# An MoE decoder step on one Trainium2 core: each expert's first matrix as one 4 MB transfer instead of two of 2 MB

## What is computed

```python
def expert_block(args):
    xb, e = args
    gu = xb @ w_e_in[e]                        # (1024, 1024): 4 MB in float32
    gt, up = jnp.split(gu, 2, axis=-1)
    return (jax.nn.silu(gt) * up) @ w_e_out[e]   # (512, 1024): 2 MB in float32

out = lax.map(expert_block, (buf.reshape(n_blocks, MOE_BLOCK, D_MODEL), block_expert)).reshape(-1, D_MODEL)
y = jnp.sum(out[dest].reshape(T, EXP_TOPK, D_MODEL).astype(f32) * gate[..., None], axis=1)
```

## Time and profile before

| | us |
|---|---|
| median of 3 runs | 1650.59 (1649.15 to 1651.14) |
| the profiled execution | 1654.85 |
| its span, first to last instruction | 1653.0 |
| stage with the experts, fetches and blocks in turn | about 1121.5 to 1612 |
| TensorE busy | 1494.1 (90% of the span) |
| chain that ended last | PE 66%, DMA 21%, DVE 6%, issue 3% |

### The profile page before, as it was taken

How to read it: one execution, slowest core, us unless ns; L and a number is a source line. 1 busy time by engine, 2 the same in 40 slices (tenths; PEclk the granted TensorE clock), 3 DMA queues, 4 the chain that set the end, 5 groups by cost and what they waited for, 6 DMA issues and landing times.

```text
span 1653.0 us, 34687 instructions
## 1 busy us (share of the span) xinstructions
PE 1494.1 (90%) x14388; PEld 1195.1 (72%) x14388; DVE 692.1 (42%) x1226; ACT 454.5 (27%) x873; POOL 170.7 (10%) x355
## 2 busy tenths in 40 slices
PE   7999899999999999999999899948887886978887
PEld 7999799999988899999888598724443443434443
DVE  5766576666688562223443243651111110101115
ACT  4533554544322641222433322111000000000000
POOL 0000000000000000000000000013232232323320
PEclk9999899999999999999999999969899998989999
DMA  5222445344457223352464726538999999699994
GB/s 205 71 82 89 112 151 152 110 145 143 148 203 268 79 90 102 119 181 89 150 226 147 280 74 252 226 163 352 421 403 422 371 421 422 254 405 419 420 389 165
DMA packets 86705, 368.64 MB, mean 223 GB/s; under 512 B 14280, under 2 KB 37520, under 8 KB 71568
## 3 DMA queue, kind: packets, MB, share of 16 engines
q1 hardware_dynamic: 80432, 357.76, 57.0%
q0 software_dynamic: 6144, 8.95, 1.5%
HBM read 345.20 MB, written 29.31 MB: 227 GB/s over the span
## 4 chain that ended last, share of the span: by engine, by line
PE 66%; DMA 21%; DVE 6%; issue 3%; ACT 2%; SPq 1%; POOL 1%; POOLq 0%; DVEq 0%; ACTq 0%
PE ps L619 33%; DMA arena<-in_w 13%; PE ps L760 5%; DMA xg<-x_dram,curg 5%; PE ps L1077 4%; PE ps L1096 4%; PE ps L973 3%; PE ps L865 3%; PE ps L847 3%; PE ps L712 1%; PE ps L709 1%; DVE cv L1650 1%; PE ps L1061 1%; PE ps L876 1%; DMA kv<-in_vc 1%
## 5 line engine op out<-in xcount | busy, mean ns | idle before, releaser
L1077 PE MATMUL ps<-arena,xT 128*32 128x256 f32 x4096 | 255.4, 402 | 55.7 <-DMA arena<-in_w 55.0
L1589 DVE TENSOR_TENSOR wl<-raw,wh 128x1024 fp32r<-128x1024 f32 x152 | 184.6, 1222 | 166.2 <-ACT wh L1154 166.0
L619 PE MATMUL ps<-xh,wh 128*128 128x272 f32 x1136 | 245.0, 297 | 5.5 <-DVE wl L1589 5.5
L1077 PEld LDWEIGHTS ps<-arena,xT 128*32 128x32 f32 x4096 | 132.7, 114 | 153.5 <-DMA arena<-in_w 42.2
L619 PE MATMUL ps<-xh,wl 128*128 128x272 f32 x1136 | 235.2, 289 | 0.0
L619 PE MATMUL ps<-xl,wh 128*128 128x272 f32 x1136 | 234.5, 288 | 0.0
L619 PEld LDWEIGHTS ps<-xh,wh 128*128 128x128 f32 x1136 | 179.6, 189 | 17.2 <-issue 13.2
L619 PEld LDWEIGHTS ps<-xl,wh 128*128 128x128 f32 x1136 | 178.7, 189 | 0.0
L619 PEld LDWEIGHTS ps<-xh,wl 128*128 128x128 f32 x1136 | 177.7, 189 | 0.0
L1154 ACT ACTIVATE wh<-raw 128x1024 fp32r<-128x1024 f32 x152 | 159.1, 1055 | 38.9 <-PE ps L973 20.8
L2232 DVE TENSOR_TENSOR hbuf<-sg,ps 128x128 f32<-128x128 f32 x64 | 18.4, 288 | 300.7 <-ACT sg L1454 235.1
(11 more groups left out here) (404 smaller groups left out, 2402.0 us busy)
## 6 DMA issues: line engine op xcount, KB each, us to landing
arena<-in_w SPq DMA_DIRECT2D x96, 2048.0 KB
raw<-in_slabs SPq DMA_DIRECT2D x152, 512.0 KB, 4.4
bc<-acs_dram SPq DMA_DIRECT2D x16, 512.0 KB, 5.8
hs<-in_h SPq DMA_DIRECT2D x16, 512.0 KB, 5.3
out_h_sample<-hs SPq DMA_DIRECT2D x16, 512.0 KB, 4.1
kv<-in_kT SPq DMA_DIRECT2D x8, 1024.0 KB, 4.8
kv<-in_vc SPq DMA_DIRECT2D x4, 1024.0 KB, 7.8
kvx<-in_vc SPq DMA_DIRECT2D x2, 2048.0 KB, 11.4
```

Of the source, the lines that this page charges most:

```text
L619: r = nc.tensor.matmul(ps[:, 2 * (ub % 2) + half, 0:HT], w[:, s, col], x[:, koff + kk, half * HT:half * HT + HT], start=first and kk == 0 ...
L1077: r = nc.tensor.matmul(ps[QS * c:QS * c + QS, 2, 0:2 * FQ], xT[:, s, kk % 2, kk // 2 * QS:kk // 2 * QS + QS], arena[:, at_:at_ + 2 * FQ], ...
L1589: v.tensor_tensor(wl[:, s], raw[:, s], wh[:, s].bitcast(F32), ALU.subtract).then_inc(w_lo, 1)
```

## The change

Each first matrix is fetched as one transfer with one semaphore, and `gate_up` waits for it once, before step 0. The same is done in the conditional part for blocks that don't fit.

```diff
-        w1_in = [[sem(f"w1_in{i}{half}") for half in range(2)] for i in range(3)]
+        w1_in = [[sem(f"w1_in{i}{half}") for half in range(1)] for i in range(3)]
...
             def fetch1(n_, e=None):
                 if n_ >= 3:
                     sp_.wait_ge(Z["gu_mm"], sum(b_ <= n_ - 3 for b_ in BLOCKS))
-                for half in range(2):
-                    at_, col = w1_at[n_ % 3] + half * (W1S // 2), slice(half * (W1S // 2), (half + 1) * (W1S // 2))
+                for half in range(1):
+                    at_, col = w1_at[n_ % 3] + half * W1S, slice(half * W1S, (half + 1) * W1S)
                     src = A["w1"][n_][:, col] if e is None else A["w1"][ds(e, 1), :, col].rearrange("o p n -> p (o n)")
-                    sp_.dma_start(arena[:, at_:at_ + W1S // 2], src).then_inc(w1_in[n_ % 3][half], 16)
+                    sp_.dma_start(arena[:, at_:at_ + W1S], src).then_inc(w1_in[n_ % 3][half], 16)
...
                 for kk in range(KT):
-                    if kk % (KT // 2) == 0:
-                        pe.wait_ge(w1_in[b_ % 3][kk // (KT // 2)], 16 * (b_ // 3 + 1) if ob is None else ix(16 * (W1_USES + 1), ob, 16))
+                    if kk == 0:
+                        pe.wait_ge(w1_in[b_ % 3][0], 16 * (b_ // 3 + 1) if ob is None else ix(16 * (W1_USES + 1), ob, 16))
```

More of the change, by code:

```diff
@@ L577, in _ @@
                     sp_.wait_ge(Z["gu_mm"], ix(NB0, ob, 1))
-                    for half in range(2):
-                        at_, col = w1_at[0] + half * (W1S // 2), slice(half * (W1S // 2), (half + 1) * (W1S // 2))
-                        sp_.dma_start(arena[:, at_:at_ + W1S // 2], A["w1"][ds(e, 1), :, col].rearrange("o p n -> p (o n)")
+                    for half in range(1):
+                        at_, col = w1_at[0] + half * W1S, slice(half * W1S, (half + 1) * W1S)
+                        sp_.dma_start(arena[:, at_:at_ + W1S], A["w1"][ds(e, 1), :, col].rearrange("o p n -> p (o n)")
                                       ).then_inc(w1_in[0][half], 16)
```

## The result

The changed kernel takes 1712.12 us (median), the kernel before 1650.87 in the same comparison. The ratio is 1.0361 with a 95% interval of 1.0327 to 1.0395: 61 us or 3.6% slower. Medians are over all executions and ratios over the fast ones alone; one of the four of the changed kernel took 8158 us and is left out of its ratio. In a second session the ratio was 1.0367 (1.0334 to 1.04). The prediction had the sign, but 1659.8 us and a range that ends at 1698. The case that it put second, slow gathers, is the one that came, and larger than it was priced.

What follows compares the result with a forecast made beforehand. The prediction took the expert stage as bound by its weight stream, with holes where late blocks delay fetches. Terms of 0.7, 1.5, 3.1, 1.7, 0.4 and 1.8 sum to +9.2 us: 1659.8 us on the median, range 1651 to 1698.

Steps and rivals of the forecast that it cites:

- slow gathers: Rival, chance 0.30: ten gathers on the chain each +3.6 us behind longer weight packets, 36 us, +45 in all: 1696.
- The signal: At first blocks of large experts, all 64 `gate_up` matmuls start only after the whole matrix lands: +9.2 us in sum.
- the seven places of the forecast: Waits for weights at 1172.43, 1221.54, 1285.37, 1400.46, 1481.61, 1527.57, 1574.70: +0.7, 1.5, 3.1, 1.7, 0.4, 0, 1.8 us.
- cold start: TensorE starting at the lower clock (1.2, not 2.4 GHz) after idling: 1.4 us taken, 0 below and 2.4 above.
- The gather behind longer packets: Gathers beside the weight stream, whose packets get twice as long: bounds 0 and +3.6 us per gather, 0 taken as likeliest.
- The rule weighed against it: Skill's rule that a DMA engine alternates queue rows at packet boundaries; with one row per packet it gives slow gathers' sum, not 9.2.
- Quicker gathers: Rival, chance 0.07: gather delay goes by number of weight packets, so 1.8 us off each of ten: -9, 1642.
- No change: Rival, chance 0.07: the later start is swallowed because blocks behind wait for gathers issued earlier; 1650 to 1653.
- A quicker stream: Rival, chance 0.03: 29 fewer seams of 0.26 us between weight transfers save at most 7.5 us, leaving +1.7: 1652.
- The prediction's 2 us for each transfer: Skill's fixed cost per weight transfer: 29 fewer would save 58 us, to 1602; the prediction said the trace doesn't agree.
- The list of what to look for: Profile after: groups of 64 about 5 us, 4096 fewer packets, full-window rate still 421 GB/s, 11 us gathers meaning slow gathers.
- The forecast of the idle time at `arena<-in_w`: At L1077, TensorE's idle time for weights rises from 97 us by some 2 us for each waiting expert.

Runs made afterwards that it cites:

- experiment 1: Against the kernel before: first matrices still as two 2 MB transfers with 16 KB packets, but one semaphore for both; 1668.8 us, ratio 1.0085.
- experiment 2: Changed kernel (one 4 MB transfer, one signal) with each row in two DRAM pieces, so runs end at 16 KB; 1665.51 us, 1.0074 of the kernel before.
- experiment 6: Kernel before with early gathers, plus one signal at 16 KB packets: 1654.65 us, ratio 0.9993; its other run, 8 KB packets and two signals: 1651.96 us.
- experiment 3: Changed kernel (one 4 MB transfer, one signal) with first matrices in 8 KB runs, second ones at 16 KB; 1662.47 us, 1.0053 of the kernel before.

## Why the prediction was wrong, step by step

**The signal** (forecast +9.2). The mechanism is right: 14 and 12 us in experiments 1 and 2, 9.3 in experiment 6. The sum holds place by place up to the last two. In experiment 1 the fetches that were issued before at 1249.58, 1317.67, 1446.58 and 1507.56 come later by 1.6, 4.5, 6.2 and 7.5 us, where the forecast's terms add up to 2.2, 5.3, 7.0 and 7.4. TensorE's first projection behind a wait for weights, with one signal (experiment 1):

```profile
1172.20 6.03 PE L1077 MATMUL ps<-arena,xT 128*32 128x256 f32 x64 [9.65 <-DMA arena<-in_w]
...
1221.24 5.35 PE L1077 MATMUL ps<-arena,xT 128*32 128x256 f32 x64 [3.98 <-DMA arena<-in_w]
...
1286.77 5.08 PE L1077 MATMUL ps<-arena,xT 128*32 128x256 f32 x64 [6.97 <-DMA arena<-in_w]
...
1406.46 4.96 PE L1077 MATMUL ps<-arena,xT 128*32 128x256 f32 x64 [7.30 <-DMA arena<-in_w]
...
1487.71 5.29 PE L1077 MATMUL ps<-arena,xT 128*32 128x256 f32 x64 [6.98 <-DMA arena<-in_w]
...
1584.52 6.37 PE L1077 MATMUL ps<-arena,xT 128*32 128x256 f32 x64 [2.09 <-DMA arena<-in_w]
```

At the seven places of the forecast (the seventh, at 1534.90, takes 5.59) the groups of 64 take 4.96 to 6.37 us against 3.66 warm. So a cold start costs 1.3 to 2.7 us, 1.9 on the mean, where 1.4 was taken and 2.4 was the upper bound. At 1285 the second half had taken 1.93 and the whole takes 5.08: +3.15 where 3.1 was written. Two places were missed. The fetch issued at 1551.93 before was put at 0, since 3.9 us of slack should swallow 3.1. It comes at 1564.62, later by 12.7, where the fetch before that in the list (1507.56) was later by 7.5: the cold group ahead of it took 5.59 where a warm half of 1.93 had stood, 3.7 more, and after a wait of 1.81 us for a gather `down` and the next group ran slow, which makes most of another 1.7. The slack swallowed only a part, for the arrival behind it goes from 1574.70 to 1584.52, later by 9.8. At the last `down` the lag is 10.6 us, against 9.2 forecast. And after the last block the layer's end is longer. Its window is 41.6 us at a granted clock of 0.79 in experiment 1, against 35.9 at 0.90 in the kernel before:

```profile
1627.70:1669.30 41.60, 31.91 (x60) 11.28 (x60) 20.93 (x31) 1.47 (x5) 1.17 (x2) 0.79 0.43 162
```

TensorE had waited there 3.2 us for the rows of `ybuf`, against 1.1 in the kernel before. The longer window is 5.7 us of this profiled execution's loss. From the last `down` to the end the other one-signal kernels with packets of 16 KB have it too (40.7 us in experiment 2, 40.1 in experiment 6); the kernel after (36.8 us at 0.90) and experiment 3 (35.3) don't, and the kernel before with early gathers stands between (38.0). The forecast had no term for it. Whether it belongs to the late signal or is chance of the alignment is not shown.

**The gather behind longer packets** (bounds 0 and +3.6 us for each, 0 taken) is the step that failed. It cost 47 of the 61 us (experiment 2 against the changed kernel), where the sum has 0. The text had the row that spoke for it, 5.46 us of delay against a packet time of 0.62, and let "no row shows a gather's time change with the packet's length" stand for evidence against. It was only a lack of evidence. The measured growth in the chain is 10.6 - 8.0 = 2.6 us on the mean, so +3.6 was too much for the mean, and right as a bound. The rival was undersized in its second factor. It multiplied by the ten gathers of the chain before; 18 were in the chain after. Presumably those joined it that had had less to spare than the growth; no view shows a gather's spare time. 18 x 2.6 us would be 47 us, just the packet's part of the loss, but that is luck, since the rest of the chain changed as well. What this makes of the chain is seen when it is cut to the stage with the experts. Shares of the chain by line, from 1098 us to the last `down`, first the kernel before (519 us):

```profile
by line: DMA arena<-in_w 42.5%; DMA xg<-x_dram,curg 15.4%; PE ps L1077 14.0%; PE ps L1096 12.6%; issue 5.7%; PE ps L1061 2.7%; SPq L540 0.9%; DVE yb L2242 0.9%; SPq L569 0.9%; SPq L546 0.8%; POOL ybuf_dram L1534 0.7%; DMA xg<-x_dram,gidx 0.
```

and the kernel after (573 us):

```profile
by line: DMA xg<-x_dram,curg 33.2%; DMA arena<-in_w 17.7%; PE ps L1096 15.8%; PE ps L1077 14.8%; issue 8.1%; PE ps L1061 3.1%; POOL ybuf_dram L1534 1.5%; DVE yb L2242 1.5%; PE ps L1084 0.7%; POOL curg L1516 0.7%; POOL curs L1531 0.6%; DMA x
```

In microseconds the gathers go from 80 to 190 and the waits for weights from 221 to 101, so these two cancel: +110 and -119. What makes the 54 us that the stage is longer is what stands around each gather in the chain. `down` (L1096) goes from 65 to 91 us, `gate_up` (L1077) from 73 to 85, "issue" from 30 to 46; the smaller lines make up for the 9 us between +110 and -119. A transfer of weights in the chain hides all that; a gather can be issued only after the `down`, the copy and the scatter ahead of it. One turn of this circle stands in the chain of the kernel after:

```profile
1357.29 11.73 DMA xg<-x_dram,curg
...
1369.76 2.97 PE ps L1096 x32
...
1372.84 0.44 DVE yb L2242
...
1376.60 8.41 DMA xg<-x_dram,curg
```

It takes 19.3 us from one gather to the next. By the code the gather of block b+4 stands behind the scatter of block b (the prediction has "the block before last"), and TensorE takes up the rows of b+4 just ahead of `down` of block b+2, so one turn is two blocks. So at most every second gather of a stretch can stand in the chain. The rival's pricing, so much more for each gather, was too simple in this as well.

**The rule weighed against it.** The Trainium skill, "DMA: Bandwidth & Descriptors", section "Queues, rings and completion order", has an engine change between queue rows at packet boundaries. The runs agree so far as they reach: with early gathers the time from issue to landing has a median of 6.3 us at 8 KB, 7.0 at 16 KB and 8.7 where two thirds of the bytes go in 32 KB, at nearly the same rate (medians of 415, 421 and 426 GB/s in full windows of 20 us). It isn't proportional to the packet, though; between 8 and 16 KB it moves by only 0.7. That a gather's wait is counted in turns is inferred from these times, no view shows a single turn.

**Quicker gathers** (0.07): excluded by the same row. **No change** (0.07): excluded by the ratio. **A quicker stream** (0.03): the full window has 433 GB/s instead of 421, but experiment 2 shows that the number of transfers isn't the reason, since its slices with the same transfers have 424 at most and its windows of 20 us 426. The length of the packet is what is left. The prediction's 2 us for each transfer stand in the Trainium skill, "DMA: Bandwidth & Descriptors", section "Anatomy of one DMA", for transfers that GpSimd issues, while SP issues the weights. With 32 transfers fewer, experiment 2 is 3 us below experiment 1, within the intervals.

**The list of what to look for** held in the groups of 64, the packets down by 4096 and some, the gathers of 11 us and more as the sign of the rival, and the stages up to 1100 us as before (the first gather at 1097.14 instead of 1099.01). It did not hold in the rate of full windows, 433 instead of 421 GB/s. The forecast of the idle time at `arena<-in_w` set out from the wrong figure: its 97 us count matmuls and weight loads, and at L1077 the matmuls alone waited 55.0 us, 22 times. Experiment 1 has, for matmuls alone:

```profile
  DMA arena<-in_w: 68.6, 14
```

That is 13.6 us more, as forecast, in 14 waits instead of 22. In the kernel after it is 40.1 us, for there the gathers hold TensorE first.

## What to carry to other kernels

Where small indirect transfers run beside a stream of large ones, the length of the stream's contiguous runs moves their latency. Look at what the small ones gate before a row is made longer, and count for a slower one all that would join the chain, not only those in it now. And the remedy was not in the stream: an order on GpSimd that issues a gather when its slot is free took some 61 us off the changed kernel and 0.5 to 0.7% off the kernel before, with the packets untouched.

## What the runs showed of the hardware

The rate of a full stream of weights on 16 engines rises with the length of a row: full slices have 402 to 407 GB/s at 4 KB, 414 to 417 at 8 KB and 419 to 424 at 16 KB. Taken in windows of 20 us with the engines at 1.00 busy or more, the medians are 405, 415, 421 to 423, and 426 to 431 where the first matrices go in 32 KB. A row of 32 KB goes as one packet (82096 packets instead of 86705). A gather beside the stream, from issue to landing, has a median of 6.3 us with rows of 8 KB, 7.0 with 16 KB and 8.7 with 32 KB for two thirds of the bytes, all with the early order; the first one, with nothing beside it, takes 2.9 to 3.1. A transfer of 4 MB and two of 2 MB that stand in the queue together took the same time, 1.0074 and 1.0085 with overlapping intervals.
